# Two parts of a modulation vector: from one fused operation on VectorE to a scale on ScalarE and an add on GpSimd

## The chip, the core and the metric

The kernel runs on one core of one Trainium2 chip. A core has five engines that the profile names PE (TensorE, the matrix multiplier), DVE (VectorE), ACT (ScalarE), POOL (GpSimd) and SP (SyncE, which here only starts transfers). All of them work on a memory of 128 partitions (SBUF); PE writes into eight banks of a second one (PSUM), and DVE and ACT read these banks. The metric is the device time of one execution in microseconds, lower is better.

## What is computed

The reference is a two-block network on 256 tokens of width 2048. The first block is modulated: a vector of six parts of 2048 numbers is made from a condition `c`, and the parts shift, scale and gate what the block does.

```
cond = jax.nn.silu(c)                                  # 2048 numbers
mod = (cond @ ada_w[l] + ada_b[l])[:, None, :]         # ada_w is 2048 x 12288, f32
sh1, sc1, g1, sh2, sc2, g2 = jnp.split(mod, 6, axis=-1)    # parts 0 to 5
...
x = x + g1 * hybrid_mixer(h, ..., w_out[l])            # ends in a product with w_out, 2048 x 2048
h = rms_norm(x, norm_ffn[l]) * (1.0 + sc2) + sh2
x = x + g2 * peer_ffn(h, peer_wq[l], ...)              # begins with q = h @ wq, 2048 x 2048
```

The change concerns parts 4 (`sc2`) and 5 (`g2`) of this vector, each of them 2048 x 2048 weights or 16 MB.

## The kernel before

**Split products.** Both projections that matter here, the product with `w_out` (function `project_residual`, called the first stage below) and the product with `peer_wq` (function `project`, the second stage), are done to f32 precision from parts of lower width. A weight tile is copied to a rounded *high half* by ACT (`split_high`, L282), and DVE subtracts that from the tile to get the *low half* (`split_low`, L299). PE then makes three products, high by high, low by high and high by low (`multiply_split`, L325 to L327). The work is cut into 4 chunks of 512 output columns, and each chunk into 8 units of 2 x 128 rows of the weight, so a stage has 32 units; a unit costs ACT one copy of 128x1024, DVE one subtraction of 128x1024, and PE 12 matmuls of 512 columns. Three units of halves are held, so ACT may be two units ahead of the one that PE works on. SP loads the weights of a chunk in four quarters into one of two buffers. In the first chunk of each stage DVE also makes the normalised columns that PE multiplies: for one unit it scales a bank (L663 in the first stage, L661 in the second), ACT makes the high half (L673) and DVE the low half (L677). After each chunk DVE takes the results from two banks, in the first stage by a product with the gate (L2309) and an addition to `x` (L2311), in the second by a copy (L871).

**Modulation beside it.** `ModulationParts` makes one part of the vector beside a stage. The 2048 columns of the part are two pieces of 1024; a piece has 16 tiles of 128 rows by 1024 columns, so there are 32 tiles of 512 KB. POOL starts their transfers into a ring of five slots (`on_pool`, L414): tile 0 at once, the others from the moment that the second quarter of the stage's weights has landed, and each once its slot is free. DVE calls `add_tile` after each unit of `split_low`, as the argument `between`: one fused instruction multiplies a tile by a column of `cond` and adds it to the piece's sum (L434; L432 for the first tile of a piece). In the end PE sums each piece over the partitions (`on_pe`, L445, 8 matmuls by a column of ones), and ACT copies the result out (`on_act`, L455). In the first stage both pieces are summed after the last chunk, in the second stage after the second and the fourth chunk; ACT's copies stand in its program at the same places.

**Order.** Each engine runs its own list of instructions in the order of the code; they wait for each other by semaphores alone. `added` counts the tiles added: it frees ring slots and lets PE sum. At the end of each stage all engines meet.

Of the kernel before, what the change touches and what calls it, by code (L numbers as in the profile page):

```python
# [17 lines left out]
ALU = mybir.AluOpType  # L18
# [28 lines left out]
class Chain:  # L47

    def __init__(self, sem):  # L50
        self.sem, self.n = sem, 0
# [148 lines left out]
class WeightStream:  # L200
# [67 lines left out]

    def split_high(self, act, kt, n, source=None):

        b, turn = self.chunk["act"] % 2, self.chunk["act"] // 2
        if source:
            source.head_act(act)
        for k in range(0, kt, self.UNIT):
            if source:
                source.highs(act, k // self.UNIT)
            self.wait_quarter(act, b, turn, k, kt)
            u = self.unit["act"]
            if u >= self.UNITS_HELD:

                act.wait_ge(self.unit_used, u - self.UNITS_HELD + 1)
            act.activation(self.high[:, u % self.UNITS_HELD, :, 0:n], self.buf[b][:, k:k + self.UNIT, 0:n],  # L282
                           ACT.Copy).then_inc(self.high_ready, 1)
            self.unit["act"] += 1
        if source:
            source.highs(act, kt)
        self.chunk["act"] += 1
# [98 lines left out]
class ModulationParts:  # L386

    def __init__(self, m, io, st, ctx, name, parts, piece=1024, ring=5, memory=None, acc=None, row=None):  # L390
        self.PIECE, self.RING = piece, ring
# [11 lines left out]
        self.biased = m.sem(name + "_biased")  # L403
        self.row_ready, self.stored = m.sem(name + "_row_ready"), m.sem(name + "_row_stored")
        self.n_add = self.n_sum = self.n_col = 0
# [11 lines left out]
    def add_tile(self, dve):  # L417
# [18 lines left out]
        ins.then_inc(self.added, 1)  # L436
        self.n_add = n + 1

    def on_pe(self, pe, banks=None):
# [357 lines left out]
def project(nc, m, st, acts, kt, w, c0, n, out, source, store=None, width=CHUNK, mod=None, asked=0, bias=None):  # L797
# [6 lines left out]
    with ExitStack() as ctx:  # L804
        m.weights.split_memory(ctx)
        with nc.Block() as block:
# [1430 lines left out]
def project_residual(nc, m, st, acts, w, source_of, gain=None, mod=None, stash=None):  # L2237

    with ExitStack() as ctx:  # L2240
# [9 lines left out]
        with nc.Block() as block:  # L2250
# [15 lines left out]
            if mod:  # L2266
                @block.gpsimd
                def _(pool):
                    mod.on_pool(pool, 0, 1)
                    pool.wait_ge(*second_quarter)  # L2270
                    mod.on_pool(pool, 1)

# [9 lines left out]
            def _(act):  # L2282
                for c, size in chunks(D):
                    m.weights.split_high(act, KD, size, source=None if c else source)
                if mod:
# [4 lines left out]
            def _(dve):  # L2290
                V = m.dve_chain.on(dve)
                work = chunks(D)
                for i in range(len(work) + 1):
                    if i < len(work):
                        m.weights.split_low(dve, KD, work[i][1], between=mod and mod.add_tile, source=None if i else source)
                    if i == 0:
# [2509 lines left out]
def whole_program(nc, io, out):  # L4806

    with ExitStack() as ctx:
# [5 lines left out]
        with ExitStack() as c1:  # L4814
# [21 lines left out]

            mod = ModulationParts(m, io, st, c1, "mod_late", (4,), memory=proj[:, 0, 0:1])
            project_residual(nc, m, st, mixed, io["w_out"][0], ssm_norm, st.mod_dram[2 * D:3 * D], mod,
# [61 lines left out]
```

## Time and profile before

| | |
|---|---|
| time, median of 3 runs | 3623.35 us (3615.46 to 3626.14) |
| the profiled execution | 3617.39 us, of which the span of its instructions is 3615.7 us |
| busy, share of the span | PE 91%, DVE 72%, ACT 35%, POOL 11% |
| first stage (`w_out`, part 4) | from 511 to 632 us of the span |
| second stage (`peer_wq`, part 5) | from 632 to 754 us of the span |
| data moved | 869.87 MB, 241 GB/s over the span |

Every engine's busy share is a mean over a dozen stages with different limits, so it says little of these two. Times in a row count from the start of the span; a row of the order of time gives start, duration, engine, line, operation, and in brackets the idle time before it and what ended that. `x8` is a count; several equal instructions in a row are merged.

### The profile page before, as it was taken

The numbers are of one execution on the slowest core, as the hardware profiler recorded it, in microseconds if no ns is written. First come the engines' busy times: TensorE is split into PE (matmuls) and PEld (weight loads), VectorE is DVE, ScalarE is ACT, GpSimd is POOL, SyncE is SP. The second block draws the span as 40 slices with busy tenths as digits, with TensorE's granted clock in tenths as the row PEclk, the third lists the DMA queues.
The fourth block names the chain that finished last, engine by engine and source line by source line (L and its number), as shares of the span: only waits on it lengthen the run. The fifth ranks groups of instructions, "written<-read, shape, count | busy, mean of one in ns | idle before, by whom it ended". The sixth has DMA issues, their size and how long they took to land. (4 is left out here: it accounts for less than half of the span.)

```text
span 3615.7 us, 46554 instructions
## 1 busy us (share of the span) xinstructions
PE 3286.2 (91%) x18835; PEld 2594.9 (72%) x18835; DVE 2599.4 (72%) x3316; ACT 1270.7 (35%) x1485; POOL 412.7 (11%) x393
## 2 busy tenths in 40 slices
PE   7979879889889998999999979998998999899998
PEld 5755647679879998877777758747884585444776
DVE  5865768889999997678878864565544654697564
ACT  3323233334445554444444433321331210201333
POOL 0011101100112122023232200001000020000000
PEclk7889889899999999999999989999999999999999
DMA  9984357947989999899999955330655312555554
GB/s 351 377 288 145 112 188 277 344 148 239 334 316 344 368 366 356 309 386 370 370 380 384 381 178 169 125 108 28 209 199 203 106 32 88 164 164 174 185 211 151
DMA packets 294494, 869.87 MB, mean 241 GB/s; under 512 B 33548, under 2 KB 108408, under 8 KB 242312
## 3 DMA queue, kind: packets, MB, share of 16 engines
q1 hardware_dynamic: 257352, 670.16, 52.7%
q0 software_dynamic: 34320, 190.40, 14.0%
q10 hardware_dynamic: 2608, 6.33, 0.5%
q8 instruction: 150, 2.46, 0.3%
q14 instruction: 64, 0.52, 0.0%
HBM read 819.77 MB, written 46.38 MB: 240 GB/s over the span
## 5 line engine op out<-in xcount | busy, mean ns | idle before, releaser
L2506 DVE TENSOR_TENSOR expert_w_low<-expert_w,expert_w_high 128x2048 fp32r<-128x2048 f32 x256 | 585.2, 2286 | 152.1 <-ACT expert_w_high L2933 149.7
L2841 PE MATMUL bank<-h_halves,expert_w_high 128*128 128x384 f32 x2048 | 610.9, 369 | 67.0 <-DVE expert_w_low L2506 66.9
L2933 ACT ACTIVATE expert_w_high<-expert_w 128x2048 fp32r<-128x2048 f32 x256 | 490.3, 1915 | 443.2 <-DMA expert_w<-in_peer_v_dram 296.0
L299 DVE TENSOR_TENSOR weights_low<-weights,weights_high 128x1024 fp32r<-128x1024 f32 (+4 forms) x288 | 338.3, 1177 | 289.9 <-ACT weights_high L282 286.5
L2842 PE MATMUL bank<-h_halves,expert_w_low 128*128 128x192 f32 x2048 | 520.2, 254 | 0.0
L282 ACT ACTIVATE weights_high<-weights 128x1024 fp32r<-128x1024 f32 (+4 forms) x288 | 293.7, 1022 | 454.4 <-PE bank L327 381.2
L2841 PEld LDWEIGHTS bank<-h_halves,expert_w_high 128*128 128x128 f32 x2048 | 393.6, 192 | 77.9 <-DVE expert_w_low L2506 77.6
L2842 PEld LDWEIGHTS bank<-h_halves,expert_w_low 128*128 128x128 f32 x2048 | 400.1, 195 | 0.0
L2910 PE MATMUL bank<-expert_w_high,gated_acts_halves 128*128 128x512 f32 x512 | 202.7, 396 | 20.4 <-DVE expert_w_low L2506 20.3
L2912 PE MATMUL bank<-expert_w_high,gated_acts_halves 128*128 128x512 f32 x512 | 200.5, 392 | 0.0
L2911 PE MATMUL bank<-expert_w_low,gated_acts_halves 128*128 128x512 f32 x512 | 200.4, 391 | 0.0
L2914 PE MATMUL bank<-expert_w_high,gated_acts_halves 128*128 128x512 f32 x512 | 199.5, 390 | 0.0
L2915 PE MATMUL bank<-expert_w_low,gated_acts_halves 128*128 128x512 f32 x512 | 199.4, 389 | 0.0
L3285 PE MATMUL bank<-s_gates_w,x_rows 128*128 128x512 f32 x448 | 197.0, 600 | 0.2 <-issue 0.2
L3285 PE MATMUL bank<-s_in_w,x_rows 128*128 128x512 f32 x384 | 172.3, 603 | 12.0 <-DMA s_in_w<-in_w_in_dram 9.4
L3285 PEld LDWEIGHTS bank<-s_gates_w,x_rows 128*128 128x128 f32 x448 | 85.1, 192 | 107.6 <-issue 107.6
L3285 PEld LDWEIGHTS bank<-s_in_w,x_rows 128*128 128x128 f32 x384 | 72.1, 192 | 101.8 <-issue 86.8
L2802 POOL DMA_INDIRECT query_area<-in_peer_v_dram,own_list x43 | 112.7, 2621 | 254.4 <-DVE choose_area L2562 247.0
L1505 PE MATMUL bank<-weights,x_rows 128*128 128x512 f32 (+1 forms) x256 | 118.5, 615 | 21.0 <-DMA weights<-in_w_in_dram 17.7
L325 PE MATMUL bank<-weights_high,branch_high 128*128 128x512 f32 x320 | 128.3, 401 | 9.8 <-DVE weights_low L299 4.9
L2910 PEld LDWEIGHTS bank<-expert_w_high,gated_acts_halves 128*128 128x128 f32 x512 | 96.6, 189 | 50.1 <-issue 30.0
L2952 ACT ACTIVATE expert_act<-bank 128x192 f32<-128x192 f32 x128 | 41.9, 328 | 242.6 <-PE bank L2842 125.3
(737 smaller groups left out, 6529.6 us busy)
## 6 DMA issues: line engine op xcount, KB each, us to landing
expert_w<-in_peer_u_dram SPq DMA_DIRECT2D x128, 1024.0 KB, 6.8
expert_w<-in_peer_v_dram SPq DMA_DIRECT2D x128, 1024.0 KB, 9.6
weights<-in_ada_w_dram SPq DMA_DIRECT2D x88, 512.0 KB, 9.9
weights<-in_w_out_dram SPq DMA_DIRECT2D x32, 1024.0 KB, 11.6
weights<-in_w_in_dram SPq DMA_DIRECT2D x32, 960.0 KB, 9.0
weights<-in_w_in_dram SPq DMA_DIRECT2D x32, 928.0 KB, 9.7
weights<-in_w_in_dram SPq DMA_DIRECT2D x56, 512.0 KB, 8.2
s_gates_w<-in_w_in_dram SPq DMA_DIRECT2D x56, 512.0 KB, 3.6
```

What stands on the lines that cost most here:

```text
L282: act.activation(self.high[:, u % self.UNITS_HELD, :, 0:n], self.buf[b][:, k:k + self.UNIT, 0:n], ACT.Copy).then_inc(self.high_ready, 1)
L299: dve.tensor_tensor(self.low[:, u % self.UNITS_HELD, :, 0:n], self.buf[b][:, k:k + self.UNIT, 0:n], self.high[:, u % self.UNITS_HELD, :, 0 ...
L2506: dve.tensor_tensor(wl[:, n % RING, :], w_sb[:, n % RING, :], wh[:, n % RING, :], ALU.subtract).then_inc(wl_ready, 1)
L2841: pe.matmul(o[:, 0:2 * DENSE], uh[:, b, k, :], acts.both[:, k, :, 0:DENSE], start=(k == 0), stop=False)
L2842: mm = pe.matmul(o[:, DENSE:2 * DENSE], ul[:, b, k, :], acts.h[:, k, 0:DENSE], start=False, stop=(k == KD - 1))
L2910: pe.matmul(bank[:, :], high, wh[:, b, cs], start=first, stop=False)
L2911: pe.matmul(bank[:, :], high, wl[:, b, cs], start=False, stop=False)
L2912: mm = pe.matmul(bank[:, :], low, wh[:, b, cs], start=False, stop=last)
L2914: pe.matmul(bank[:, :], both, wh[:, b, cs], start=first, stop=False)
L2915: mm = pe.matmul(bank[:, :], both, wl[:, b, cs], start=False, stop=last)
L2933: act.activation(wh[:, n % RING, :], w_sb[:, n % RING, :], ACT.Copy).then_inc(wh_ready, 1)
L3285: mm = pe.matmul(self.both[tt][:, :], self.whole[:, p * self.UNIT + u, tt * P:(tt + 1) * P], self.w[:, n % self.HELD, u, :], start=first, ...
```

## The change

DVE's `add_tile` is called no more in these two stages. ACT multiplies each tile by its column of `cond` in place, in the ring slot (`scale_tile`, L451 of the kernel after): it does so after the high half of each unit but the first of a chunk, and twice after the last. POOL adds the scaled tile to the sum (`add_scaled`, L478; L476, a product with ones, for the first tile of a piece), and its program now alternates a transfer and an addition (`load_and_add`). A new semaphore `scaled` goes from ACT to POOL; `added` now comes from POOL itself. The other stage that uses `add_tile` keeps it. `scale_by_gpsimd` is not called. The argument `stores_row` only leaves out two semaphores.

```diff
@@ split_high (ACT)
             act.activation(self.high[:, u % self.UNITS_HELD, :, 0:n], self.buf[b][:, k:k + self.UNIT, 0:n],
                            ACT.Copy).then_inc(self.high_ready, 1)
             self.unit["act"] += 1
+            if between and k:
+                between(act)
@@ ModulationParts
+    def scale_tile(self, act):
+        n = self.n_scaled
+        if n == self.tiles:
+            return
+        self.scaled = self.m.sem(self.name + "_scaled")
+        tile, k = self.ring[:, n % self.RING, :], n % KD
+        act.wait_ge(self.loaded[n % self.RING], 16 * (n // self.RING + 1))
+        act.activation(tile, tile, ACT.Copy, scale=self.st.cond[:, k:k + 1]).then_inc(self.scaled, 1)
+        self.n_scaled = n + 1
+
+    def add_scaled(self, pool, by_act):
+        n = self.n_add
+        piece, k = divmod(n, KD)
+        a, tile = self.acc[:, piece % 2, :], self.ring[:, n % self.RING, :]
...
+        if by_act:
+            pool.wait_ge(self.m.sem(self.name + "_scaled"), n + 1)
+        if n:
+            pool.wait_ge(self.added, n)
+        if k == 0:
+            pool.tensor_tensor(a, tile, view(self.st.ones[:, 0:1], [[0, self.PIECE]]), ALU.mult).then_inc(self.added, 1)
+        else:
+            pool.tensor_tensor(a, a, tile, ALU.add).then_inc(self.added, 1)
+        self.n_add = n + 1
+
+    def load_and_add(self, pool, scale=False):
+        for n in range(self.tiles):
+            m = n + self.RING - 1
+            if n and m < self.tiles:
+                self.on_pool(pool, m, m + 1)
+            if scale:
+                self.scale_by_gpsimd(pool)
+            self.add_scaled(pool, not scale)
@@ project and project_residual, POOL
                     mod.on_pool(pool, 0, 1)
                     pool.wait_ge(*second_quarter)
-                    mod.on_pool(pool, 1)
+                    mod.on_pool(pool, 1, mod.RING)
+                    mod.load_and_add(pool)
@@ project, ACT (project_residual alike)
                 for i, (c, size) in enumerate(work):
-                    m.weights.split_high(act, kt, size, source=source if i == 0 else None)
+                    m.weights.split_high(act, kt, size, source=source if i == 0 else None, between=mod and mod.scale_tile)
+                    if mod:
+                        mod.scale_tile(act)
                     if mod and i % 2:
                         mod.on_act(act)
@@ project, DVE (project_residual alike)
                     if c is not None:
-                        m.weights.split_low(dve, kt, size, source=source if i == 0 else None, between=mod and mod.add_tile)
+                        m.weights.split_low(dve, kt, size, source=source if i == 0 else None)
```

On DVE, before, at the start of the first stage: each low half (L299) is followed by the fused operation on a tile (L432, L434; the ring and the sums lie in memory named `projection_rows`).

```order
L299 TENSOR_TENSOR weights_low<-weights,weights_high 128x1024
L432 TENSOR_SCALAR projection_rows<-projection_rows,cond 128x1024
L299 TENSOR_TENSOR weights_low<-weights,weights_high 128x1024
L434 SCALAR_TENSOR_TENSOR projection_rows<-projection_rows,cond 128x1024
L299 TENSOR_TENSOR weights_low<-weights,weights_high 128x1024
L434 SCALAR_TENSOR_TENSOR projection_rows<-projection_rows,cond 128x1024
L299 TENSOR_TENSOR weights_low<-weights,weights_high 128x1024
L663 TENSOR_SCALAR ssm_norm_whole<-bank,vector_columns 128x256 x2
L434 SCALAR_TENSOR_TENSOR projection_rows<-projection_rows,cond 128x1024
```

The same place after (L301 is the low half, L715 the scaled bank, L729 the low half of the columns).

```order
L301 TENSOR_TENSOR weights_low<-weights,weights_high 128x1024 x4
L715 TENSOR_SCALAR ssm_norm_whole<-bank,vector_columns 128x256 x2
L301 TENSOR_TENSOR weights_low<-weights,weights_high 128x1024
L715 TENSOR_SCALAR ssm_norm_whole<-bank,vector_columns 128x256 x2
L729 TENSOR_TENSOR mixed_low<-ssm_norm_whole,mixed_high 128x512
```

The fused operations are gone, and the four low halves of the first units follow one another.

On POOL, before, from the end of the first stage to the second: all 32 transfers of tiles stand in a row, and nothing else is done in the second stage.

```order
L414 DMA projection_rows<-in_ada_w_dram 128x1024 x32
L2250 UNCONDITIONAL_BRANCH
L156 ISA x2
L833 UNCONDITIONAL_BRANCH
L414 DMA mod_last_ring<-in_ada_w_dram 128x1024 x32
```

The same place after, from the last five additions of the first stage on (`mod_last_acc` is the sum of part 5).

```order
L478 TENSOR_TENSOR projection_rows<-projection_rows 128x1024 x5
L2305 UNCONDITIONAL_BRANCH
L156 ISA x2
L885 UNCONDITIONAL_BRANCH
L418 DMA mod_last_ring<-in_ada_w_dram 128x1024 x5
L476 TENSOR_TENSOR mod_last_acc<-mod_last_ring,ones_col 128x1024
L418 DMA mod_last_ring<-in_ada_w_dram 128x1024
L478 TENSOR_TENSOR mod_last_acc<-mod_last_acc,mod_last_ring 128x1024
L418 DMA mod_last_ring<-in_ada_w_dram 128x1024
```

The transfer of tile n+4 now stands ahead of the addition of tile n, and the next transfer behind it.

On ACT, before, at the start of the second stage: three high halves of weights, then those of the first three pairs of columns (L673).

```order
L635 ACTIVATE norm_rms<-norm_ms 128x2
L282 ACTIVATE weights_high<-weights_2 128x1024 x3
L673 ACTIVATE h_halves<-norm_whole 128x2x256 x3
L282 ACTIVATE weights_high<-weights_2 128x1024
L673 ACTIVATE h_halves<-norm_whole 128x2x256
```

The same place after.

```order
L282 ACTIVATE weights_high<-weights_2 128x1024 x2
L451 ACTIVATE mod_last_ring<-mod_last_ring,cond 128x1024
L282 ACTIVATE weights_high<-weights_2 128x1024
L451 ACTIVATE mod_last_ring<-mod_last_ring,cond 128x1024
L725 ACTIVATE h_halves<-norm_whole 128x2x256 x3
L282 ACTIVATE weights_high<-weights_2 128x1024
```

The scaling of tiles 0 and 1 now stands ahead of the first columns' high halves.

## Rows read from the trace of the kernel before

**Rows 1.** Windows: busy time (and count) of each engine, granted clock, transfers.

```profile
core 0: us, PE busy (x) PEld busy (x) DVE busy (x) ACT busy (x) POOL busy (x), PEclk, DMA share, GB/s
527.00:532.00 5.00, 0.23 (x2) 0.10 (x1) 2.58 (x3) 1.06 (x1) 0.53 (x1) 0.86 1.00 401
540.00:557.00 17.00, 13.98 (x57) 10.01 (x55) 16.45 (x21) 6.30 (x8) 2.64 (x5) 1.00 1.03 403
557.00:624.00 67.00, 66.14 (x289) 53.89 (x289) 63.83 (x62) 23.38 (x22) 10.06 (x19) 1.00 0.77 286
704.00:752.00 48.00, 47.63 (x198) 37.75 (x198) 40.18 (x37) 14.12 (x14) 5.82 (x11) 0.96 0.50 163
```

**Rows 2.** Groups by line, 511 to 632: count | busy us, mean ns | idle before.

```profile
L299 DVE TENSOR_TENSOR weights_low<-weights,weights_high 128x1024 fp32r<-128x1024 f32 x32 | 39.0, 1220 | 2.2 <-ACT weights_high L282 1.9
L434 DVE SCALAR_TENSOR_TENSOR projection_rows<-projection_rows,cond 128x1024 f32<-128x1024 f32 x30 | 38.3, 1278 | 8.7 <-DMA projection_rows<-in_ada_w_dram 8.5 <-issue 0.2
L282 ACT ACTIVATE weights_high<-weights 128x1024 fp32r<-128x1024 f32 x32 | 33.8, 1059 | 47.8 <-PE bank L327 39.6 <-PEq L331 5.5 <-DMA weights<-in_w_out_dram 2.7
L414 POOL DMA_DIRECT2D projection_rows<-in_ada_w_dram x32 | 16.9, 530 | 144.0 <-DVE projection_rows L434 66.2 <-POOLq L2169 65.0 <-DMA weights<-in_w_out_dram 8.6
L2311 DVE TENSOR_TENSOR x_rows<-x_rows,residual_tmp 128x512 f32<-128x512 f32 x8 | 5.5, 692 | 0.5
```

**Rows 3.** Groups by line, 632 to 754.

```profile
L299 DVE TENSOR_TENSOR weights_low<-weights,weights_high 128x1024 fp32r<-128x1024 f32 x32 | 39.1, 1222 | 12.8 <-ACT weights_high L282 12.5
L677 DVE TENSOR_TENSOR h_halves<-norm_whole,h_halves 128x512 fp32r<-128x512 f32 x8 | 5.5, 692 | 1.0 <-ACT h_halves L673 0.2
```

**Rows 4.** Order of time: the first wait for a tile in both stages.

```profile
529.42 1.28 DVE L434 SCALAR_TENSOR_TENSOR projection_rows<-projection_rows,cond 128x1024 f32<-128x1024 f32 x1 [8.46 <-DMA projection_rows<-in_ada_w_dram]
531.00 0.53 POOL L414 DMA_DIRECT2D projection_rows<-in_ada_w_dram  x1 [7.54 <-DVE projection_rows L434]
...
643.44 0.50 PE L325 MATMUL bank<-weights_high,h_halves 128*128 128x512 f32 x1 [0.54 <-DVE h_halves L677]
...
649.54 1.28 DVE L434 SCALAR_TENSOR_TENSOR mod_last_acc<-mod_last_ring,cond,mod_last_acc 128x1024 f32<-128x1024 f32 x1 [2.63 <-DMA mod_last_ring<-in_ada_w_dram]
```

**Rows 5.** Order of time in the first stage's last chunk.

```profile
613.06 1.06 ACT L282 ACTIVATE weights_high<-weights 128x1024 fp32r<-128x1024 f32 x1 [1.72 <-PE bank L327]
614.15 1.23 DVE L299 TENSOR_TENSOR weights_low<-weights,weights_high 128x1024 fp32r<-128x1024 f32 x1 [0.29 <-ACT weights_high L282]
```

**Rows 6.** Order of time: a 128x1024 operation on POOL, and DVE beside it.

```profile
2444.93 0.98 DVE L3131 TENSOR_TENSOR weights<-bank,block_ident 128x256 f32<-128x256 f32 x2 [5.89 <-PE bank L3072]
2445.09 2.34 POOL L3548 TENSOR_TENSOR weights<-weights,incl_mask 128x1024 f32<-128x1024 f32 x1
```

**Rows 7.** Order of time in the expert stage: gathers on POOL, and DVE beside them.

```profile
1427.60 0.93 POOL L2802 DMA_INDIRECT query_area<-in_peer_v_dram,own_list  x1 [0.30 <-issue]
...
1712.46 2.28 DVE L2506 TENSOR_TENSOR expert_w_low<-expert_w,expert_w_high 128x2048 fp32r<-128x2048 f32 x1
1712.81 2.74 POOL L2802 DMA_INDIRECT query_area<-in_peer_v_dram,own_list  x1 [4.79 <-DVE choose_area L2562]
...
1807.68 3.68 POOL L2802 DMA_INDIRECT query_area<-in_peer_v_dram,own_list  x1 [4.80 <-DVE choose_area L2562]
1810.13 0.41 DVE L2519 TENSOR_TENSOR gated_acts_halves<-choose_area,gated_acts_halves 128x256 fp32r<-128x256 f32 x1
```

**Rows 8.** Order of time: PE's sums of the pieces, and what follows.

```profile
623.95 5.46 PE L445 MATMUL bank<-ones_col,projection_rows 128*128 128x1 f32 x32
...
699.03 1.94 PE L445 MATMUL bank<-ones_col,mod_last_acc 128*128 128x1 f32 x16
701.35 2.95 ACT L282 ACTIVATE weights_high<-weights 128x1024 fp32r<-128x1024 f32 x3 [0.17 <-issue]
703.81 0.77 PE L325 MATMUL bank<-weights_high,h_halves 128*128 128x512 f32 x1 [2.84 <-DVE weights_low L299]
...
751.42 1.94 PE L445 MATMUL bank<-ones_col,mod_last_acc 128*128 128x1 f32 x16
```

More of the change, by code:

```diff
@@ L267, in seen, with split_high @@
             self.chunk[e] += 1
-    def split_high(self, act, kt, n, source=None):
+    def split_high(self, act, kt, n, source=None, between=None):
         b, turn = self.chunk["act"] % 2, self.chunk["act"] // 2
@@ L386, with __init__ @@
 class ModulationParts:
-    def __init__(self, m, io, st, ctx, name, parts, piece=1024, ring=5, memory=None, acc=None, row=None):
+    def __init__(self, m, io, st, ctx, name, parts, piece=1024, ring=5, memory=None, acc=None, row=None, stores_row=True):
         self.PIECE, self.RING = piece, ring
@@ L403, in __init__ @@
         self.biased = m.sem(name + "_biased")
-        self.row_ready, self.stored = m.sem(name + "_row_ready"), m.sem(name + "_row_stored")
+        if stores_row:
+            self.row_ready, self.stored = m.sem(name + "_row_ready"), m.sem(name + "_row_stored")
+        self.name, self.n_scaled = name, 0
         self.n_add = self.n_sum = self.n_col = 0
@@ L437, in add_tile, with scale_by_gpsimd @@
         self.n_add = n + 1
+    def scale_tile(self, act):
[7 more added lines that the diff above has]
+        self.n_scaled = n + 1
+    def scale_by_gpsimd(self, pool):
+        n = self.n_scaled
+        tile, k = self.ring[:, n % self.RING, :], n % KD
+        pool.wait_ge(self.loaded[n % self.RING], 16 * (n // self.RING + 1))
+        self.m.pool_chain.on(pool)(pool.tensor_tensor(tile, tile, view(self.st.cond[:, k:k + 1], [[0, self.PIECE]]), ALU.mult))
+        self.n_scaled = n + 1
+    def add_scaled(self, pool, by_act):
+        n = self.n_add
+        piece, k = divmod(n, KD)
+        a, tile = self.acc[:, piece % 2, :], self.ring[:, n % self.RING, :]
+        if k == 0 and piece >= 2:
+            pool.wait_ge(self.summed, piece - 1)
+        if by_act:
[15 more added lines that the diff above has]
+            self.add_scaled(pool, not scale)
     def on_pe(self, pe, banks=None):
@@ L2270, in _ @@
                     pool.wait_ge(*second_quarter)
-                    mod.on_pool(pool, 1)
+                    mod.on_pool(pool, 1, mod.RING)
+                    mod.load_and_add(pool)
             @block.tensor
@@ L2283, in _ @@
                 for c, size in chunks(D):
-                    m.weights.split_high(act, KD, size, source=None if c else source)
+                    m.weights.split_high(act, KD, size, source=None if c else source, between=mod and mod.scale_tile)
+                    if mod:
+                        mod.scale_tile(act)
                 if mod:
@@ L2294, in _ @@
                     if i < len(work):
-                        m.weights.split_low(dve, KD, work[i][1], between=mod and mod.add_tile, source=None if i else source)
+                        m.weights.split_low(dve, KD, work[i][1], source=None if i else source)
                     if i == 0:
@@ L4835, in ssm_norm @@
                                      rows, lambda tt: squares[:, :], groups=2, k0=HALF // P)
-            mod = ModulationParts(m, io, st, c1, "mod_late", (4,), memory=proj[:, 0, 0:1])
+            mod = ModulationParts(m, io, st, c1, "mod_late", (4,), memory=proj[:, 0, 0:1], stores_row=False)
             project_residual(nc, m, st, mixed, io["w_out"][0], ssm_norm, st.mod_dram[2 * D:3 * D], mod,
```

## The prediction

> **What bounds the kernel now.** I read the windows of the two stages first, since the page's shares are means over other stages too. Once the first chunk is past, both stages run at PE's pace: from 557 to 624 PE is busy 66.14 of 67.00 us, from 704 to 752 it is 47.63 of 48.00 [rows 1]. The first of these holds chunks two to four of the first stage, 24 units, so a unit takes 67.00/24 = 2.79 us. DVE looks nearly as full (63.83 of 67), but the order of time shows that it is not the bound: ACT waits 1.72 us for PE to give back halves, and DVE then waits 0.29 us for ACT [rows 5]. So the fused operations, 1.28 us each [rows 2], lie in time that DVE has.
>
> DVE costs PE time in the first chunks only. Tile 1 lands at 529.42, DVE has stood 8.46 us at its fused operation by then [rows 4], and the low half of unit 2 stands behind it, so PE does 0.23 us of work between 527 and 532. Until 557 DVE, with the normalised columns, is busy 16.45 of 17 us and PE 13.98 [rows 1]. In the second stage tile 1 comes at 649.54, when PE has been at work since 643.44 [rows 4].
>
> **The change, part by part.** *Removed from DVE:* 30 fused operations of 1.28 us a stage [rows 2] and two cheaper first ones. Away from the first chunk PE sets the pace, so this gives nothing there. In the first chunk the most to be had is the hole of 4.8 us (5.00 less 0.23) and the 3.0 us that PE idles until 557 [rows 1].
>
> *Added to ACT:* 32 scalings a stage. The nearest row is its copy of the same shape, 1.06 us [rows 2]. ACT then works 2.12 us per unit of 2.79, so the work itself is hidden. Its place is not: ACT now waits for tile 1 where DVE did. In the first stage three high halves are made by then, which takes away the hole. In the second stage the high halves of the first columns stand behind the scaling of tile 1, and without them PE has nothing: its start moves from 643.44 to past 649.54 + 1.06 = 650.6 [rows 4].
>
> *Added to POOL:* 32 additions a stage. The one shape in this trace with the same size and two inputs took 2.34 us [rows 6]. Around it POOL issues a transfer, 0.53 us [rows 2], and needs about 0.30 us from an end to the next issue (529.42 + 1.28 = 530.70, issue at 531.00 [rows 4]). So POOL alone needs 2.34 + 0.53 + 0.30 = 3.17 us a tile, more than PE's 2.79 for a unit, and there is one tile per unit.
>
> The Trainium skill says that it does (SBUF — State Buffer, Who interferes with whom): a VectorE instruction with two inputs in SBUF and a GpSimd instruction that reads SBUF use one read interface, and whichever comes first holds it for the whole instruction. For POOL's side the gathers agree (2.74 us against 0.93); no run here shows DVE's side. By this rule the sum is that of the next paragraph, without it that of the first rival.
>
> Bounds per tile are therefore 3.17 us (nothing waits) and 2.34 + 1.22 = 3.56 us (additions and low halves strictly take turns). I take turns, because the only rows with both kinds at once show no overlap at all, not a partial one. While POOL does its 0.83 us between two additions, DVE's 1.22 fits; then POOL's next addition is ready; so what takes turns is busy all the time, and I can simply add it up.
>
> First stage. From 529.42 + 1.06 = 530.5 on: 31 additions x 2.34 = 72.5; low halves of units 3 to 31, 29 x 1.22 = 35.4 [rows 2]; the columns' four low halves and eight L2311, 12 x 0.69 = 8.3 [rows 2, 3]. Together 116.2, so the last addition ends at 646.7. PE, done by about then, needs 0.3 and half of 5.46 us for the second sum: 649.7. Before, the sums ended at 623.95 + 5.46 = 629.4 [rows 8]. That is **20.3 us more**.
>
> Second stage. From 650.6 on: 72.5, then 31 low halves 37.8 and eight of columns 5.5 [rows 3], together 115.8: 766.4. In its middle everything stands in a line: after the second chunk PE can sum only behind the 16th addition, ACT's copy of that sum stands ahead of the next high half, and the next low half behind that. There nothing takes turns for 0.83 between the last two additions, 1.94 of sum, 0.38 to ACT's next high half (699.03 + 1.94 to 701.35) and 1.06 for it [rows 2, 8], 4.2 in all: 770.6. With the last sum of 1.94 it is 772.5; before it was 751.42 + 1.94 = 753.4 [rows 8]. That is **19.1 us more**.
>
> The sum is 39.4 us, on the profiled execution's own 3617.4: **3657 us**. The median of the runs is 6 us above that execution, so from there it would be 3663; I write 3658. A turn can be cheaper, as the gathers' 0.81 instead of 0.93 show (0.12 each in some 120 turns: 14 us less), or dearer, by the 0.30 from an end to POOL's issue at POOL's 62 turns (19 us more): 3643 to 3676 for this case.
>
> **The rivals.** *Only POOL waits.* If DVE passes a running addition, PE keeps 2.79, and POOL adds to its 3.17 a wait for the low half that it may meet: 1.22/2.79 = 0.44 of the time, 0.61 on average, so 0.27, in all 3.44. The first stage's last addition ends at 530.5 + 27 x 3.44 + 4 x 2.91 (no transfer) = 635.0, its sums at 638.0, 8.6 more. The second: 650.6 + 104.5 + 4.7 (the middle: the sum 1.94, 0.38, two high halves and a scaling of 1.06 before tile 16 can be added, less POOL's own 0.83) + 1.94 = 761.7, 8.3 more: 3634 us. For it: PE and ACT have slack to hide behind. Against: only that the gathers and subtractions show no partial overlap [rows 7].
>
> *Not slower: nothing waits.* Then POOL's 3.17 alone decides: 530.5 + 27 x 3.17 + 4 x 2.64 = 626.7 and 629.7 with the sum, against 629.4; in the second stage 650.6 + 96.2 + 4.7 + 1.94 = 753.4, against 753.4. PE gains its hole of 4.8 us and then waits for the last additions: 3617 us. This holds as long as a tile costs POOL no more than about 3.2 us. Against it speak the gathers. It also shows why a gain is far off: even with free operands the additions end no earlier than PE does now, and all that DVE costs PE in the first chunks, 4.8 + 3.0 = 7.8 us, is under 0.3%.
>
> *The clock falls too.* With turns PE works 2.79 of each 3.56 us, 78%. If the granted clock went to its lower level, a unit would take up to 5.6 us, 2.0 more than a turn; over half of 60 units that is 60 us: about 3717. Against it: from 540 to 557 PE worked 13.98 of 17 us, 82%, in pieces, and the clock was 1.00 [rows 1].
>
> **How the numbers follow.** Turns 0.73, only POOL waits 0.12, nothing waits 0.08, turns with a fallen clock 0.05, a real gain 0.02. A difference of 0.3% is 11 us, about what a measurement of this kernel can tell from none. Turns and the fallen clock are slower, and so is most of the case in which only POOL waits (17 us more): 0.73 + 0.05 + 0.10 = 0.88. No change takes the rest of that and the case in which nothing waits: 0.10. Faster keeps 0.02. The range reaches from 3630, to take in the case in which only POOL waits, to 3680, above the dearest turn: it leaves out the last three cases and little more.
>
> **What would show it.** In the profile after: an addition on POOL lasts 2.3 us by itself and up to 1.2 more where it begins in a low half; a low half lasts up to 2.3 us more than 1.22 (or starts so much late) where it begins in an addition; a unit takes about 3.6 us in the later chunks, and PE waits for low halves there, where now it waits for nothing; the clock stays at 1.00 there; ACT waits for tile 1 at the start of both stages; the last POOL addition ends some 17 us or more after today's end of PE's products, and PE's sums wait for it. The forecast is wrong if low halves keep 1.22 us and their pace of 2.79 beside additions: then the first or second rival holds, told apart by whether additions last 2.3 us throughout. It is wrong the other way if PE's clock falls, or if tiles come so late that ACT waits for transfers all along.

## The result: 0.95% slower, with the profile after

The changed kernel takes 3654.24 us (median of 4 runs, 3650.63 to 3659.47) against 3619.72 us of the kernel before, timed beside it: a ratio of 1.0095, with a 95% interval from 1.0073 to 1.0117. The profiled execution took 3650.63 us, of which the span is 3648.9.

A yardstick serves for all kernels below. A stage is measured from PE's first weight load (first stage) or the copy of part 4's last sum (second stage) to the start of ACT's copy of the stage's last sum. Before, these three times were 519.29, 629.44 and 753.40, so the stages took 110.15 and 123.96 us. After, they are 516.33, 643.20 and 782.44: 126.87 and 139.24 us, so 16.7 and 15.3 more. The two profiled executions differ by 33.2 us, so 32.0 of these lie in the two stages. The forecast was 3658.

The groups by line of the kernel after, the first stage (511 to 645), in the columns of [rows 2]:

```profile
L301 DVE TENSOR_TENSOR weights_low<-weights,weights_high 128x1024 fp32r<-128x1024 f32 x32 | 76.5, 2416 | 22.9 <-ACT weights_high L282 22.5
L478 POOL TENSOR_TENSOR projection_rows<-projection_rows 128x1024 f32<-128x1024 f32 x30 | 76.0, 2534 | 17.6 <-ACT projection_rows L451 16.5
L451 ACT ACTIVATE projection_rows<-projection_rows,cond 128x1024 f32<-128x1024 f32 x32 | 36.1, 1138 | 7.8 <-DMA projection_rows<-in_ada_w_dram 7.8
L2369 DVE TENSOR_TENSOR x_rows<-x_rows,residual_tmp 128x512 f32<-128x512 f32 x8 | 14.4, 1798 | 0.5
```

The low half (L301) has doubled, from 1220 ns in [rows 2] to 2416; so has the addition to `x` (L2369), from 692 to 1798. POOL's addition takes 2534 ns, where the one in [rows 6] took 2.34 us. The scaling is 1138 ns, not 1060. Next the windows that answer to [rows 1], and one more:

```profile
core 0: us, PE busy (x) PEld busy (x) DVE busy (x) ACT busy (x) POOL busy (x), PEclk, DMA share, GB/s
527.00:532.00 5.00, 3.29 (x22) 2.78 (x21) 4.18 (x4) 4.52 (x6) 4.68 (x3) 1.00 1.03 400
540.00:557.00 17.00, 12.12 (x48) 8.52 (x48) 16.59 (x13) 9.44 (x10) 12.66 (x9) 0.96 1.03 404
557.00:624.00 67.00, 53.92 (x214) 43.26 (x214) 54.21 (x27) 36.66 (x36) 52.28 (x35) 0.90 0.74 260
580.00:590.00 10.00, 6.53 (x17) 5.20 (x18) 7.76 (x3) 1.04 (x2) 5.77 (x5) 0.66 1.04 395
```

The hole between 527 and 532 is gone (PE 3.29 us of 5, before 0.23), but from 557 to 624 PE works 53.92 of 67 us where it worked 66.14. How POOL and DVE meet is seen in the order of time at the start of the third chunk, first POOL's rows, then DVE's:

```profile
591.15 2.40 POOL L478 TENSOR_TENSOR projection_rows<-projection_rows 128x1024 f32<-128x1024 f32 x1 [4.75 <-ACT projection_rows L451]
593.85 0.57 POOL L418 DMA_DIRECT2D projection_rows<-in_ada_w_dram  x1 [0.30 <-POOL projection_rows L478]
594.44 2.46 POOL L478 TENSOR_TENSOR projection_rows<-projection_rows 128x1024 f32<-128x1024 f32 x1
...
597.79 2.46 POOL L478 TENSOR_TENSOR projection_rows<-projection_rows 128x1024 f32<-128x1024 f32 x1
```

```profile
590.05 1.23 DVE L301 TENSOR_TENSOR weights_low<-weights,weights_high 128x1024 fp32r<-128x1024 f32 x1 [2.30 <-ACT weights_high L282]
592.95 1.69 DVE L301 TENSOR_TENSOR weights_low<-weights,weights_high 128x1024 fp32r<-128x1024 f32 x1 [1.67 <-ACT weights_high L282]
595.61 2.38 DVE L301 TENSOR_TENSOR weights_low<-weights,weights_high 128x1024 fp32r<-128x1024 f32 x1 [0.97 <-ACT weights_high L282]
598.39 6.29 DVE L301 TENSOR_TENSOR weights_low<-weights,weights_high 128x1024 fp32r<-128x1024 f32 x2 [0.40 <-ACT weights_high L282]
```

The additions end at 593.55, 596.90 and 600.25. The low halves begun inside the first two end at 592.95 + 1.69 = 594.64 and 597.99: each 1.09 us after the addition's end, however much earlier it began (0.60 and 1.29). A low half thus does 0.13 of its 1.22 us beside an addition and then stands still. The addition of 594.44 begins 0.20 us before a low half's end (594.64) and lasts 2.46, so it waits 0.12 of these 0.20 and does 0.08 of its 2.34 us meanwhile. Additions follow each other by 597.79 - 594.44 = 3.35 us, which is 2.34 - 0.08 and 1.22 - 0.13. Three more places in the order of time: PE at the same chunk's start, POOL's last five additions of the stage, and ACT's waits for tile 1 in both stages:

```profile
583.47 0.77 PE L327 MATMUL bank<-weights_high,mixed_high 128*128 128x512 f32 x1 [6.48 <-DVE weights_low L301]
```

```profile
625.50 15.28 POOL L478 TENSOR_TENSOR projection_rows<-projection_rows 128x1024 f32<-128x1024 f32 x5
```

```profile
525.55 1.16 ACT L451 ACTIVATE projection_rows<-projection_rows,cond 128x1024 f32<-128x1024 f32 x1 [6.94 <-DMA projection_rows<-in_ada_w_dram]
...
662.35 1.15 ACT L451 ACTIVATE mod_last_ring<-mod_last_ring,cond 128x1024 f32<-128x1024 f32 x1 [5.81 <-DMA mod_last_ring<-in_ada_w_dram]
```

PE stands 6.48 us ahead of the third chunk and restarts at the lower clock (0.66 from 580 to 590, that is partly at 1.2 of 2.4 GHz). The last five additions, with no transfer between them, end at 640.78. While low halves stand against them they still begin 3.35 us apart (628.12, 631.47 and 634.82).

### The profile page after: what moved, and what is told of

It is laid out like the page before. It is cut to its first block and busy times, and to the rows that moved or that the text cites. A ratio compares the mean times of both kernels' runs of the same rounds, so it can differ in the third digit from the quotient of the medians.

```text
span 3648.9 us, 46618 instructions
## 1 busy us (share of the span) xinstructions
PE 3296.4 (90%) x18835; PEld 2603.4 (71%) x18835; DVE 2616.9 (72%) x3252; ACT 1338.3 (37%) x1549; POOL 575.7 (16%) x457
## 3 DMA queue, kind: packets, MB, share of 16 engines
q8 instruction: 150, 2.46, 0.3%
## 5 line engine op out<-in xcount | busy, mean ns | idle before, releaser
L301 DVE TENSOR_TENSOR weights_low<-weights,weights_high 128x1024 fp32r<-128x1024 f32 (+4 forms) x288 | 407.5, 1423 | 315.9 <-ACT weights_high L282 312.1
L3109 POOL TENSOR_TENSOR weights<-weights,level_masks 128x512 f32<-128x512 f32 x26 | 32.3, 1266 | 625.1 <-DVEq L3748 409.1
```

What stands on the lines that cost most here:

```text
L301: dve.tensor_tensor(self.low[:, u % self.UNITS_HELD, :, 0:n], self.buf[b][:, k:k + self.UNIT, 0:n], self.high[:, u % self.UNITS_HELD, :, 0 ...
```

## The experiments

All medians and ratios are against the kernel before, timed on the same chip beside them; interval in brackets. Stage lengths are by the yardstick, from the three times given.

| run | median, before | ratio | the three times | stages |
|---|---|---|---|---|
| x1_no_add | 3620.43, 3621.48 | 1.0004 [0.9989, 1.0019] | 517.96, 626.67, 751.57 | 108.7, 124.9 |
| x2_memset | 3623.44, 3621.48 | 1.0007 [0.9991, 1.0024] | 515.48, 625.16, 753.28 | 109.7, 128.1 |
| x3_no_reload | 3652.96, 3621.48 | 1.0100 [1.0067, 1.0132] | 517.29, 640.93, 779.64 | 123.6, 138.7 |
| x5_copy | 3644.41, 3621.48 | 1.0077 [1.0051, 1.0103] | 518.72, 640.64, 779.07 | 121.9, 138.4 |
| x6_scale_ahead | 3666.57, 3619.24 | 1.0127 [1.0110, 1.0145] | 521.52, 655.39, 799.17 | 133.9, 143.8 |
| x7_no_add_no_reload | 3610.34, 3619.24 | 0.9980 [0.9965, 0.9994] | 521.55, 621.31, 747.71 | 99.8, 126.4 |
| x8_no_residual_add | 3650.05, 3619.46 | 1.0089 [1.0057, 1.0122] | 521.15, 639.91, 779.66 | 118.8, 139.8 |
| x4_first_only | 3640.88, 3619.46 | 1.0066 [1.0044, 1.0087] | 522.28, 649.34, 773.59 | 127.1, 124.3 |
| b1_late_adds | 3604.38, 3619.24 | 0.9955 [0.9939, 0.9970] | 522.67, 621.89, 737.63 | 99.2, 115.7 |
| b2_tiles_behind_weights | 3596.40, 3619.24 | 0.9942 [0.9927, 0.9957] | 516.49, 615.77, 731.33 | 99.3, 115.6 |

**x1_no_add.** The theory is turns: a POOL addition and a DVE instruction with two inputs in SBUF exclude each other. The rivals are POOL's own pace and ACT's place. First the additions are taken away and all else is left.

```diff
-            pool.tensor_tensor(a, tile, view(self.st.ones[:, 0:1], [[0, self.PIECE]]), ALU.mult).then_inc(self.added, 1)
+            pool.memset(a, 0.0).then_inc(self.added, 1)
         else:
-            pool.tensor_tensor(a, a, tile, ALU.add).then_inc(self.added, 1)
+            pool.memset(a[:, 0:8], 0.0).then_inc(self.added, 1)
```

> Leaves out the additions of parts 4 and 5: POOL clears 8 columns where it added, everything else stays as in the changed kernel. Turns (an addition on POOL and a DVE instruction with two inputs in SBUF exclude each other, one turn is 3.35 us): low halves are back at 1.22 us, units at 2.79, and what is left is ACT's place: the hole of 4.8 us and the 3.0 us of the first stage gone, the start of the second stage later by some 7; 3610 to 3625 us against 3620 before. POOL's own pace (a tile costs POOL 3.2 us whatever it reads): the same, since POOL has nothing left to do. ACT's place (the scalings in ACT's order hold up high halves, contention matters little): still 20 us or more slower than before.

The time is that of before (1.0004). What ACT's place costs and what DVE's freedom brings come to nothing together, so ACT's place is not what costs 35 us: that rival falls. But it should have been the best case: DVE makes no additions here. PE does work 16.74 of 17 us from 540 to 557 (13.98 in [rows 1]), and then loses it again, in the order of time on ACT and on PE:

```profile
572.27 2.00 ACT L282 ACTIVATE weights_high<-weights 128x1024 fp32r<-128x1024 f32 x2 [8.58 <-DMA weights<-in_w_out_dram]
```

```profile
574.73 0.77 PE L327 MATMUL bank<-weights_high,mixed_high 128*128 128x512 f32 x1 [6.05 <-DVE weights_low L301]
```

The third chunk's weights have not landed when PE gets to them. Two windows over that time, and behind them the kernel before over the first of the two:

```profile
515.00:590.00 75.00, 63.74 (x264) 51.28 (x265) 36.91 (x43) 48.07 (x49) 17.11 (x46) 0.91 1.03 399
540.00:557.00 17.00, 16.74 (x74) 13.40 (x73) 9.19 (x9) 13.48 (x14) 3.81 (x12) 1.00 1.04 402
```

```profile
515.00:590.00 75.00, 62.42 (x254) 49.28 (x255) 59.80 (x64) 26.21 (x28) 13.19 (x25) 0.90 1.03 399
```

The transfers move 399 GB/s over these 75 us, with a share of 1.03: they never rest, weights and tiles together. They did not rest in the kernel before either.

**x2_memset.** POOL is kept as busy as by an addition, without reading.

```diff
-            pool.tensor_tensor(a, a, tile, ALU.add).then_inc(self.added, 1)
+            self.m.pool_chain.on(pool)(pool.memset(a, 0.0))
+            self.m.pool_chain.on(pool)(pool.memset(tile, 0.0))
+            pool.memset(a[:, 0:256], 0.0).then_inc(self.added, 1)
... (the first tile of a piece alike)
```

> Leaves out the additions of parts 4 and 5: POOL writes zeros to the sum and to the tile (1024, 1024 and 256 columns) in about the 2.46 us of an addition, and reads nothing; transfers and scalings stay, so POOL's period is about the same 3.3 us. Turns, and only reading takes part in them: low halves 1.22 us, PE's units 2.79; POOL ends last by some us in each stage, about 3628 us against 3620 before. Turns in which writing takes part too: low halves 2.4 us, as slow as the changed kernel (3650 or more). POOL's own pace: also 3645 to 3655, but with low halves of 1.22 us.

The first stage by line:

```profile
L301 DVE TENSOR_TENSOR weights_low<-weights,weights_high 128x1024 fp32r<-128x1024 f32 x32 | 38.8, 1224 | 45.0 <-ACT weights_high L282 44.7
L480 POOL MEMSET projection_rows<- 128x1024 f32 x30 | 29.1, 971 | 4.9 <-ACT projection_rows L451 4.4
L481 POOL MEMSET projection_rows<- 128x1024 f32 x30 | 28.7, 955 | 1.7
L482 POOL MEMSET projection_rows<- 128x256 f32 x30 | 9.4, 313 | 1.7
```

Low halves are back at 1224 ns beside 2.24 us of writing per tile, and the time is that of before. So POOL's occupation alone is not the cause: against x1_no_add it costs 3.2 us in the second stage (128.1 against 124.9) and 1.0 in the first. The cost comes with POOL's reading.

**x3_no_reload.** Transfers of the later tiles are left out, so POOL's own pace is 0.57 us faster.

```diff
-            if n and m < self.tiles:
+            if n and m < self.RING:
...
+        if n < self.RING:
+            act.wait_ge(self.loaded[n % self.RING], 16)
+        else:
+            act.wait_ge(self.added, n - self.RING + 1)
```

> Leaves out the transfers of tiles 5 to 31 in both stages: the five tiles of the ring are scaled and added again and again. POOL's period loses the issue of 0.57 us. Turns: a turn stays 3.35 us (2.27 of the addition and 1.08 of the low half), as in the last five additions of the changed kernel, so the time stays within 6 us of the changed kernel's 3654. POOL's own pace: a tile costs 2.34 + 0.15 us, less than PE's 2.79, and the time falls to 3625 or less.

The time stays at 3653. Five additions in the second chunk, two of them by themselves, and three low halves:

```profile
560.73 16.27 POOL L481 TENSOR_TENSOR projection_rows<-projection_rows 128x1024 f32<-128x1024 f32 x5 [0.47 <-ACT projection_rows L454]
...
567.10 3.21 POOL L481 TENSOR_TENSOR projection_rows<-projection_rows 128x1024 f32<-128x1024 f32 x1
570.45 3.21 POOL L481 TENSOR_TENSOR projection_rows<-projection_rows 128x1024 f32<-128x1024 f32 x1
```

```profile
565.09 9.65 DVE L301 TENSOR_TENSOR weights_low<-weights,weights_high 128x1024 fp32r<-128x1024 f32 x3 [0.40 <-ACT weights_high L282]
```

An addition takes 3.21 us, not 2.34: POOL now stands in its instruction where it issued a transfer before, and the three low halves still take 3.22 each (9.65/3). The additions begin 570.45 - 567.10 = 3.35 us apart, so a turn is as long without the transfer as with it. This rules out POOL's own pace.

**x5_copy.** Two copies with one input each take the addition's place.

```diff
-            pool.tensor_tensor(a, a, tile, ALU.add).then_inc(self.added, 1)
+            self.m.pool_chain.on(pool)(pool.tensor_copy(a, tile))
+            pool.tensor_copy(a, tile).then_inc(self.added, 1)
... (the first tile of a piece alike)
```

> Leaves out the additions of parts 4 and 5: POOL copies the tile to the sum twice, one input in SBUF instead of two. Turns in which any read of POOL takes part: low halves stretched by as long as the copies last, the time between before and the changed kernel by the share of POOL's busy time. Turns only between instructions with two inputs each: low halves 1.22 us and a time near that of the run in which POOL writes zeros. POOL's own pace: decided by the length of the copies alone, low halves 1.22 us.

Both sides wait, in the order of time on POOL and on DVE:

```profile
555.41 1.05 POOL L479 COPY projection_rows<-projection_rows 128x1024 f32<-128x1024 f32 x1
556.52 1.93 POOL L480 COPY projection_rows<-projection_rows 128x1024 f32<-128x1024 f32 x1
```

```profile
555.01 2.54 DVE L301 TENSOR_TENSOR weights_low<-weights,weights_high 128x1024 fp32r<-128x1024 f32 x1 [2.43 <-ACT weights_high L282]
```

The low half ends at 557.55, 1.09 after the first copy's end (556.46); the second copy begins at 556.52, stands until the low half is nearly done and ends at 558.45, 0.90 after it. So one input on POOL's side is enough. A low half loses less to a copy of 1.05 than to an addition of 2.34 (its mean is 1546 ns in the first stage), but two copies with their waits are as long for POOL as an addition (1176 and 1491 ns on average, against 2534), and both stages end on POOL: PE's last sum begins 0.05 us after POOL's last copy (637.03 and 636.98, 775.59 and 775.54).

**x6_scale_ahead.** POOL waits 4.75 us at 591.15 (above) and 4.59 at 622.23 for ACT's scaling, which there stands behind a high half that waits for PE. ACT now scales ahead of the high half.

```diff
+        ahead = between and source is None
...
+            if ahead:
+                between(act)
...
-            if between and k:
+            if between and k and not ahead:
... (the extra scaling after a chunk's last unit stays in the first chunk alone)
```

> Computes the same as the changed kernel. From the second chunk of a stage on ACT scales the tile ahead of each high half, not behind it. If POOL's two waits of some 4.7 us a stage at the starts of chunks come from the place of the scaling in ACT's order, they shrink to under 1 us and the additions of the first stage end some 7 us sooner, close to 32 turns of 3.35 us; with the second stage 10 to 14 us less than the changed kernel, 3640 to 3645 us. If they come from PE, which is late by itself there, POOL's waits go on to other tiles and the time stays within 4 us of 3654.

A miss: 3666.57 us, 12 more than the changed kernel, not 10 less. The wait has moved on and grown, and PE runs dry just as before:

```profile
603.57 2.40 POOL L481 TENSOR_TENSOR projection_rows<-projection_rows 128x1024 f32<-128x1024 f32 x1 [7.84 <-ACT projection_rows L454]
```

```profile
596.11 0.76 PE L330 MATMUL bank<-weights_high,mixed_high 128*128 128x512 f32 x1 [6.93 <-DVE weights_low L304]
```

So PE is late there by itself, and scaling ahead only lets POOL take more turns before DVE: the mean low half of the first stage goes from 2416 to 2607 ns. That this accounts for all of the 12 us is argued, not shown.

**x8_no_residual_add.** What makes PE late at a chunk's start? DVE's list for a chunk holds eight low halves and two additions to `x` (L2369; two, not the four of the expectation below: 8 in the stage), all with two inputs in SBUF, against eight additions on POOL.

```diff
-                        dve.tensor_tensor(xs, xs, tmp[:, tt, :], ALU.add)
+                        if not mod:
+                            dve.tensor_tensor(xs, xs, tmp[:, tt, :], ALU.add)
```

> Leaves out the addition of the first stage's product to x (DVE's second operation of each eviction, with two inputs in SBUF, 1.8 us each beside POOL's additions); all else as in the changed kernel. If POOL's waits of 4.75 and 4.59 us at the starts of the third and fourth chunk come from DVE, which has eight low halves and four such additions to put through against eight additions of POOL, and so lets PE run dry and restart at the lower clock, both waits go below 2 us, PE's wait of 6.48 us before the third chunk below 3, and the first stage is some 8 to 12 us shorter, the time about 3643. If they come from the double scaling at the end of a chunk alone, they stay above 4 us and the first stage keeps its length to 3 us.

All waits of POOL and of PE from 565 to 642 (us in total, times, longest):

```profile
POOL projection_rows L418 <- POOL projection_rows L478: 5.0, 17, 0.3
POOL projection_rows L418 <- POOL projection_rows L476: 0.3, 1, 0.3
```

```profile
PE bank L327 <- DVE weights_low L301: 4.9, 15, 0.4
```

In the changed kernel, from 565 to 645, POOL's waits for ACT and PE's for low halves were:

```profile
POOL projection_rows L478 <- ACT projection_rows L451: 9.3, 2, 4.8
PE bank L327 <- DVE weights_low L301: 13.1, 2, 6.6
```

Both of POOL's waits for ACT and PE's two long ones are gone, PE's clock from 564 to 592 is 1.00 where it was 0.88, and the first stage is 126.87 - 118.76 = 8.1 us shorter. So the additions to `x`, 1.8 us each beside POOL's, made these waits. The median (3650) fell by 4 only, where 11 were expected, and its interval holds the changed kernel's ratio of 1.0095.

**x4_first_only.** The change in the first stage, the second as before.

```diff
-                        mod.on_pool(pool, 1, mod.RING)
-                        mod.load_and_add(pool)
+                        mod.on_pool(pool, 1)
...
-                        m.weights.split_low(dve, kt, size, source=source if i == 0 else None)
+                        m.weights.split_low(dve, kt, size, source=source if i == 0 else None, between=mod and mod.add_tile)
... (ACT's scalings of the second stage go too)
```

> The change in the first stage alone; the second stage as before. If the two stages pay apart from each other: 16 to 18 us more than before, half of the changed kernel's ratio, 1.0045, and the second stage keeps its 121.6 us from ACT's first copy to the last sum's copy. If the first stage's delay is partly taken back in the second (weights and tiles that have landed in the meantime): less, 10 us or below.

The stages take 127.1 and 124.3 us: the first as in the changed kernel, the second as before. The parts pay apart. The ratio means 16 to 31 us by its interval, which just holds the expected 17.

**x7_no_add_no_reload.** The run without additions, and without the 27 later tiles.

```diff
-            if n and m < self.tiles:
+            if n and m < self.RING:
...
-            pool.tensor_tensor(a, a, tile, ALU.add).then_inc(self.added, 1)
+            pool.memset(a[:, 0:8], 0.0).then_inc(self.added, 1)
... (ACT's waits as in x3_no_reload)
```

> Leaves out the additions of parts 4 and 5 and the transfers of tiles 5 to 31. In the run without additions PE's hole of 4.8 us in the first stage was gone, but ACT waited 8.6 us for weights at 563.7 and PE 6.05 us, while the transfers moved 400 GB/s without a break from 515 to 590. If the transfers take back what the hole gives, then without the 27 tiles that wait is gone and the products of the first stage end 5 to 6 us sooner than in that run; some 3614 us against 3620. If the wait has another cause (SP's order, the release of a buffer), it stays.

The window in which PE stood 6.05 us in x1_no_add:

```profile
557.00:590.00 33.00, 32.74 (x145) 26.81 (x144) 18.02 (x18) 25.60 (x26) 2.15 (x13) 1.00 0.51 184
```

PE is full and the first stage takes 99.8 us, 10.4 less than before and 8.9 less than in x1_no_add, where 5 to 6 were expected. The transfers had taken the hole back; that is shown. The second stage is 1.5 us longer than in x1_no_add, which no run explains.

**b1_late_adds and b2_tiles_behind_weights.** If the transfers decide, the kernel before can gain by order alone: DVE's additions (and with them the release of ring slots) four units later, and both sums of the second stage at its end.

```diff
+    LATE = 4
+    def add_late(self, dve):
+        self.n_calls = getattr(self, "n_calls", 0) + 1
+        if self.n_calls > self.LATE:
+            self.add_tile(dve)
+    def add_rest(self, dve):
+        for _ in range(self.LATE):
+            self.add_tile(dve)
...
-                    if mod and i % 2:
-                        mod.on_pe(pe)
+                if mod:
+                    mod.on_pe(pe)
+                    mod.on_pe(pe)
...
-                        m.weights.split_low(dve, kt, size, source=source if i == 0 else None, between=mod and mod.add_tile)
+                        m.weights.split_low(dve, kt, size, source=source if i == 0 else None, between=mod and mod.add_late)
+                        if mod and i == len(work) - 1:
+                            mod.add_rest(dve)
... (ACT's copies of the sums and the first stage's DVE alike)
```

> The kernel before, computing the same: DVE adds each tile four units later (the last four behind the last low half), so that no low half of the first chunk stands behind a tile that has not landed, and in the second stage both sums stand at the end as in the first. The transfers bound the first stage's middle: each tile from the fifth on is fetched four units later, which gives the weights of the third chunk 2 MB or 5 us at 400 GB/s, so here PE can keep some 5 us of its hole; in the second stage the gap of 2.8 us at the middle goes. Expected 6 to 11 us less than before, 3609 to 3614. If the hole is given back as in the run without additions: within 3 us of before.

The second of the two also starts tiles 1 to 4 later:

```diff
-    second_quarter = m.weights.next_quarter(1)
+    second_quarter = m.weights.next_quarter(3)
... (the first stage alike)
```

> As the run with late additions, and tiles 1 to 4 are fetched once the fourth quarter of the first chunk's weights has landed, not the second. Transfers bound: PE's first chunk comes a few us sooner, or the same, as the tiles are only needed four units later: 0 to 4 us less than the run with late additions. If tiles then come too late for the additions, DVE waits for them and the time is longer.

Both beat both kernels: 0.9955 and 0.9942 of before. Windows of b2_tiles_behind_weights, which answer to [rows 1]:

```profile
527.00:532.00 5.00, 5.00 (x32) 4.18 (x30) 4.23 (x8) 2.61 (x4) 0.00 (x0) 1.00 1.03 400
540.00:557.00 17.00, 16.74 (x73) 13.29 (x72) 16.86 (x15) 6.08 (x6) 3.70 (x7) 1.00 1.03 406
557.00:610.00 53.00, 52.45 (x231) 42.83 (x230) 50.03 (x47) 18.37 (x18) 9.53 (x18) 1.00 0.93 340
```

PE has no hole left in these windows, though DVE makes all its additions (50.03 of 53 us busy). The stages are 10.9 and 8.4 us shorter than before, more than expected (6 to 11 in all). The two differ by no more than their intervals, and their stages are equal to 0.2 us, so the later start of four tiles is not shown to matter. What they share is three steps at once (later additions, later slots, and in the second stage the place of the sums); which of them gives how much is not separated.

## Why the prediction was right, step by step

- **Turns** hold, on both sides: x2_memset and x3_no_reload exclude POOL's own pace, x1_no_add excludes ACT's place. The Trainium skill states the two conditions (SBUF — State Buffer, Who interferes with whom): a VectorE instruction with two SBUF inputs contends with a GpSimd instruction that reads SBUF, and not with one that only writes it. The traces agree: low halves of 2416 ns beside additions, 1224 beside memsets. The prediction's "no overlap at all" reads the gathers too strongly: DVE's next instruction with two inputs in SBUF ran its usual 0.68 us (1714.66 to 1715.34) before the gather of 1712.81 ended at 1715.55. So no row of before had DVE's side; the rows after show it, as in the low half that ends at 594.64, 1.09 us after an addition.
- **The size of a turn was off**: 3.56 us in the prediction, 3.35 measured. The 0.13 that a low half does beside the addition and the 0.08 of POOL's start lie beside the other engine's work. The prediction's lower bound allowed 0.12 at each of some 120 changes of turn, which is 0.24 for an addition and a low half, so the 0.21 lies inside it.
- **"What takes turns is busy all the time"** failed, but cheaply. In the first stage 31 additions go from 526.80 to 640.78, 114.0 us, where 116.2 were forecast. Of these 12.5 are POOL's waits for ACT (4.75, 4.59 and 0.49, 1.69, 0.95 in the first chunk); the rest is 101.5, or 3.27 each. Three sizes nearly cancel, and that is luck. POOL's waits add 12.5. Turns shorter by 0.21 take off 31 x 0.21 = 6.5. And ten of the 41 DVE instructions that the sum puts into turns, 10.6 us of work, lie wholly or mostly in POOL's waits or after its last addition (the low half of 590.05 above is one). That gives 111.6; the other 2.4 are not traced. The step gives 2.2 of the 3.6 us by which the first stage's term (20.3) exceeds the 16.7 measured; tile 1 came 0.9 sooner after ACT's start of the stage (525.55 - 508.36 against 529.42 - 511.32), and the last sum 0.6 sooner after the last addition (2.4 against 3.0). The second stage's term was 19.1, measured 15.3: from the end of tile 1's scaling to the last addition it is 116.9 us (663.50 to 780.40) where 120.0 were forecast, and tile 1 again came 0.9 sooner.
- **The stalls at the chunks' starts in the first stage** belong to the additions to `x` (x8_no_residual_add). The prediction counted these (L2311) as turns of 0.69 but not what they do in DVE's list: they bring the next chunk's first low half so late that PE runs dry. PE's clock then falls, which was forecast to stay at 1.00: 0.66 from 580 to 590, 0.90 from 557 to 624. By the prediction's own list of signs this one speaks against it. In the second stage POOL's longest waits for ACT are 7.02 us for tile 2 and 4.65 in the middle, for which the sum had 4.2.
- **ACT's wait for tile 1** came in both stages (6.94 us until 525.55, 5.81 until 662.35), and the last addition ends 16.8 us after PE's products ended before (640.78 against 623.95 in [rows 8]), or 19.8 when both are counted from their stage's start. Some 17 or more were forecast.
- **The number came out better than the sum.** The terms add up to 39.4 us, and the stages measured 32.0. The forecast of 3658 still lies within 4 us of the median (3654.24), because it was set 5 us below what the sum gives from the median before (3663). That closeness is luck.
- **One step was wrong without deciding**: that PE would keep its hole of 4.8 us, and that all DVE costs in the first chunks is 7.8. With no additions at all x1_no_add gains nothing in its time and 1.4 us in the first stage, since the transfers, full until 590, then make PE wait for weights; ordered otherwise, b2_tiles_behind_weights gains 19.3 us in both stages. The row for it stood in [rows 1]: a DMA share of 1.03 at 403 GB/s from 540 to 557.

## What to carry to other kernels

Before work goes from VectorE to GpSimd, look at what VectorE keeps: if that has two inputs in SBUF and GpSimd's part reads SBUF, the two excluded each other here, and an addition of 2.34 us and a subtraction of 1.22 took 3.35 us together. POOL's memsets, which only write, left the subtraction at 1.22. And before an engine is relieved to close a hole on another, look whether the transfers are full there. Here they were, and relieving VectorE of its additions gave nothing (x1_no_add, 1.0004), while additions and transfers of tiles four units later, with both sums at the second stage's end, gave 0.9955.

## What the hardware showed that was not expected

An earlier start in the profile does not always win a turn. In x5_copy a low half begins 0.40 us ahead of a copy (555.01 and 555.41) and still ends 1.09 us after it, as if it had not begun. In the changed kernel, DVE and POOL in the order of time:

```profile
536.28 3.90 DVE L301 TENSOR_TENSOR weights_low<-weights,weights_high 128x1024 fp32r<-128x1024 f32 x1
```

```profile
536.70 2.39 POOL L478 TENSOR_TENSOR projection_rows<-projection_rows 128x1024 f32<-128x1024 f32 x1
...
552.19 2.75 POOL L478 TENSOR_TENSOR projection_rows<-projection_rows 128x1024 f32<-128x1024 f32 x1 [1.69 <-ACT projection_rows L451]
```

Two rows of its second stage:

```profile
691.14 1.21 DVE L301 TENSOR_TENSOR weights_low<-weights,weights_high 128x1024 fp32r<-128x1024 f32 x1
```

```profile
691.56 3.07 POOL L478 TENSOR_TENSOR mod_last_acc<-mod_last_acc,mod_last_ring 128x1024 f32<-128x1024 f32 x1
```

The first low half begins 0.42 us ahead of the first addition, which takes no more than its 2.39, and ends at 540.18, 1.09 after it. Another low half begins at 551.47, 0.72 ahead of the second addition, and here POOL waits (2.75). In the second stage the same lead of 0.42 is enough: the low half of 691.14 runs through in 1.21, and the addition takes 3.07. In x3_no_reload, where no transfer stands ahead of the addition, 0.03 is enough (688.86 and 688.89). So the recorded starts do not tell who wins such a near tie; what does, these runs do not settle.
